# A softmax attention over eight head pairs: scores two pairs ahead, and another order of the same instructions on three engines

## The reference, cut to what matters

```python
# q: 16 heads, k and v: 2 heads (8 query heads share one), window 128, S = 256
s = jnp.einsum('bqgrd,bkgd->bgrqk', qi, ki).astype(jnp.float32) * scale
mask = (diff >= 0) & (diff < window) & (kpos[None, :] >= 0)
s = jnp.where(mask, s, NEG)
sk = sinks.astype(jnp.float32)[None, :, :, None, None]
m = jnp.maximum(jnp.max(s, axis=-1, keepdims=True), sk)
e = jnp.exp(s - m)
p = e / (jnp.sum(e, axis=-1, keepdims=True) + jnp.exp(sk - m))
o = jnp.einsum('bgrqk,bkgd->bqgrd', p.astype(vi.dtype), vi)
```

## Time and profile before

| | |
|---|---|
| median of three runs | 2857.96 us |
| the profiled execution | 2862.86 us, span 2861.1 us |
| its mean granted TensorE clock | 0.895 |
| TensorE matmuls busy | 2506.4 us (88% of the span) |
| TensorE weight loads busy | 1733.8 us (61%) |
| VectorE busy | 1243.3 us (43%) |
| ScalarE busy | 748.5 us (26%) |
| the attention that is changed, first scores to first matmul of the projection behind it | 2591.60 to 2640.20 us, 48.60 us |

### The profile page before, as it was taken

How to read it: one execution, slowest core, us unless ns; L and a number is a source line. 1 busy time by engine, 2 the same in 40 slices (tenths; PEclk the granted TensorE clock), 3 DMA queues, 4 the chain that set the end, 5 groups by cost and what they waited for, 6 DMA issues and landing times.

```text
span 2861.1 us, 34960 instructions
## 1 busy us (share of the span) xinstructions
PE 2506.4 (88%) x14300; PEld 1733.8 (61%) x14300; DVE 1243.3 (43%) x1829; ACT 748.5 (26%) x1087; POOL 21.6 (1%) x38
## 2 busy tenths in 40 slices
PE   6999777667776677799989999999989999997998
PEld 4988222112221222178677998788957888885887
DVE  2365100000000000033533776876576778775676
ACT  4332000000000000013222334434254334345333
POOL 1000000000000000000000000000000000000000
PEclk9999877777777776799899999999989999998999
DMA  8668999999999999954333554554403545551553
GB/s 314 233 244 309 416 416 418 418 418 418 416 417 418 419 419 416 416 186 162 125 118 132 191 176 165 174 199 168 148 30 119 201 166 201 181 177 60 172 181 118
DMA packets 272100, 720.69 MB, mean 252 GB/s; under 512 B 11216, under 2 KB 128992, under 8 KB 238848
## 3 DMA queue, kind: packets, MB, share of 16 engines
q1 hardware_dynamic: 270000, 708.88, 65.6%
q0 software_dynamic: 2000, 10.38, 1.0%
HBM read 716.08 MB, written 3.15 MB: 251 GB/s over the span
## 4 chain that ended last, share of the span: by engine, by line
PE 56%; DMA 18%; SPq 12%; issue 8%; DVE 3%; ACT 2%; POOL 0%; DVEq 0%; POOLq 0%; ACTq 0%
SPq L730 12%; PE bank L1329 9%; PE bank L938 7%; DMA ring<-in_w_gate_e 6%; PE bank L872 5%; PE bank L873 5%; PE bank L874 5%; DMA A<-in_w_gate_e 5%; PE bank L1330 4%; DMA xn<-in_w_up_e 4%; PE bank_pair L872 4%; PE bank_pair L873 4%; PE bank_pair L874 4%; PE bank L1143 1%; PE bank L1129 1%
## 5 line engine op out<-in xcount | busy, mean ns | idle before, releaser
L1330 PE MATMUL bank<-HT_r,ring_r 128*128 128x256 f32 x1408 | 395.9, 281 | 0.0
L1330 PEld LDWEIGHTS bank<-HT_r,ring_r 128*128 128x128 f32 x1408 | 266.8, 190 | 0.7
L2341 DVE TENSOR_TENSOR A<-bank,A 128x512 f32<-128x512 f32 x16 | 11.1, 692 | 587.6 <-PE bank L1143 587.6
L874 PE MATMUL bank<-HT_r,ring_r 128*128 128x256 f32 x904 | 255.7, 283 | 0.0
L1329 PE MATMUL bank<-HT_r,AB_r 128*128 128x512 f32 x640 | 229.7, 402 | 1.4 <-DVE HT_r L2090 1.4
L1329 PE MATMUL bank<-HT_r,AC_r 128*128 128x512 f32 x640 | 226.7, 398 | 0.0
L2082 DVE TENSOR_TENSOR ring_r<-ring,AB_r 128x2048 fp32r<-128x2048 f32 (+1 forms) x80 | 177.5, 2260 | 101.3 <-ACT AB_r L1659 101.3
L1143 PE MATMUL bank<-ring,A 128*32 128x512 f32 x768 | 141.6, 827 | 85.0 <-DMA ring<-in_w_gate_e 50.1
L2082 DVE TENSOR_TENSOR ring_r<-ring,A_r 128x2048 fp32r<-128x2048 f32 (+1 forms) x82 | 175.8, 2182 | 15.3 <-ACT A_r L1659 15.3
L874 PE MATMUL bank_pair<-A_r 128*128 128x512 f32 x456 | 178.4, 391 | 0.0
L1659 ACT ACTIVATE AB_r<-ring 128x2048 fp32r<-128x2048 f32 (+1 forms) x80 | 146.7, 1882 | 109.0 <-DMA ring<-in_w_up 36.5
(11 more groups left out here) (480 smaller groups left out, 4472.5 us busy)
## 6 DMA issues: line engine op xcount, KB each, us to landing
ring<-in_ffn_w_gu SPq DMA_DIRECT2D x88, 1024.0 KB, 6.7
ring<-in_w_up_e SPq DMA_DIRECT2D x48, 1024.0 KB, 26.6
ring<-in_w_gate_e SPq DMA_DIRECT2D x48, 1024.0 KB, 22.3
ring<-in_w_down_e SPq DMA_DIRECT2D x48, 1024.0 KB, 19.9
ring<-in_w_in SPq DMA_DIRECT2D x46, 1024.0 KB, 7.4
ring<-in_ffn_w_down SPq DMA_DIRECT2D x40, 1024.0 KB, 6.2
A<-in_w_gate_e SPq DMA_DIRECT2D x32, 1024.0 KB, 18.9
A<-in_w_up_e SPq DMA_DIRECT2D x32, 1024.0 KB, 26.7
```

The source lines that it names most:

```text
L874: return mm(out_, lhs[1], rhs[0], start=False, stop=stop, skip_group_check=True)
L1330: last = mm(both[:, 1, :], low, h_high[:, k, :], start=False, stop=(k == DC - 1), skip_group_check=True)
```

## The change

The number of instructions and every instruction stay as they are. On TensorE, scores(1) stands before the loop, and in the loop come turn(m), scores(m + 2), product(m). On ScalarE, exps(0) and exps(1) stand before the loop, and in it come copy(m), high(m), exps(m + 2). On VectorE, max(1) stands before the loop, behind the rotation, and in it come weigh(m), max(m + 2), rest(m - 1). `swa_at` and the letters of the plan follow.

```diff
--- before.py
+++ after.py
@@ -183,8 +183,10 @@
 def swa_at(m, part, i=0):
 
     if part == "scores":
-        return 4 * m - 4
-    return 4 * m + (1 if m < 7 else 0) + (i if part == "turned" else 2)
+        return 0 if m == 1 else 4 * m - 5
+    if part == "turned":
+        return 1 + 4 * min(m, 6) + 3 * max(m - 6, 0) + i
+    return swa_at(m, "turned") + (3 if m < 6 else 2)
 
 
 Q_AT, Q_ROPE_AT = (0, 1, 2, 6), (3, 4, 5)
@@ -279,7 +281,7 @@
             p.add("swa_q", "W" * 7, [1, 6], split=2)
             p.add("swa_scores0", "A")
             p.add("swa_rope3", "W")
-            p.add("swa_heads", ("A" + "WWW") * 7 + "WWW")
+            p.add("swa_heads", "A" + "WWAW" * 6 + "WWW" * 2)
             p.add("swa_out", "AA", [0, 1], split=2)
     return p
 
@@ -1585,14 +1587,15 @@
         swa_scores(0)
         copied(pe, "swa_q", Q_AT[3])
         rope("swa_rope3", 0, pairs(q3, 3))
+        swa_scores(1)
         for m in range(8):
             g = m // 4
-            if m < 7:
-                swa_scores(m + 1)
             pe.wait_ge(S["p3_ready"], 16 + m + 1)
             for d in range(2):
                 b = open_bank("swa_heads", swa_at(m, "turned", d))
                 batch(causal_blocks(b, lambda t: p3[2 * (m % 2) + t][:, d, :]))
+            if m < 6:
+                swa_scores(m + 2)
             b = open_bank("swa_heads", swa_at(m, "out"))
             for d in range(2):
                 copied(pe, "swa_heads", swa_at(m, "turned", d))
@@ -1985,14 +1988,15 @@
             run(sk[:, m % 2, :, :], sk[:, m % 2, :, :], ACT.Exp)
             exps(m % 2, (0, m % 2), 2 * (m % 2), 16 + m + 1)
 
-        swa_exps(0)
+        for m in range(2):
+            swa_exps(m)
         for m in range(8):
             for d in range(2):
                 copy_out("swa_heads", swa_at(m, "turned", d), pT3[d][:, :], n=384)
-            if m < 7:
-                swa_exps(m + 1)
             filled(act, "swa_heads", swa_at(m, "out"))
             run(o_high[:, m, :], work_bank("swa_heads", swa_at(m, "out"))[:, 0:T], ACT.Copy).then_inc(S["o_high"], 1)
+            if m < 6:
+                swa_exps(m + 2)
             if m >= 6:
                 high("swa_out", m - 6)
         ffn3(3, 11, "swa_heads", swa_at(7, "out"))
@@ -2829,14 +2833,15 @@
 
         swa_max(0)
         turned_q("swa_q", 3, "swa_rope3", 0)
+        swa_max(1)
         for m in range(8):
             rw = rw3[:, 0, m % 2, :, :]
             dve.wait_ge(S["exp3_done"], 16 + m + 1)
             link(v.tensor_tensor(rw, rs3[:, 0, m % 2, :, :], sk[:, m % 2, :, :], ALU.add))
             link(v.reciprocal(rw, rw))
             weigh((0, m % 2), 2 * (m % 2))
-            if m < 7:
-                swa_max(m + 1)
+            if m < 6:
+                swa_max(m + 2)
             if m:
                 attention_low("swa_heads", swa_at(m - 1, "out"), 8 + m, m - 1)
         low("swa_out", 0)
```

## The result

The changed kernel takes 2873.77 us (median of four runs, 2872.15 to 2877.58), against 2857.80 for the kernel before in the same session: a ratio of 1.0051, 95% interval 1.0040 to 1.0063. It is slower by half a per cent: 16.0 us between the two medians, 14.6 us by the ratio. The profiled execution has a span of 2873.1 us, 12.0 more than before.

A forecast was written before the change was run, and what follows sets the result against it. The prediction took a ring of waits across engines in the attention, none of them full, as the bound. Six rings +8.75, head +1.3 and tail 0 gave +10.0 us on the median: 2868.0 us, range 2862.5 to 2873.0.

The forecast's parts named there:

- The ring: Attention: weigh(m), turn(m), scores(m + 2), max(m + 2), rest(m - 1), weigh(m + 1) close a new one-pair ring.
- look-ahead pays: Rival, attention: the new one-pair ring does not bind; 3.66 us a pair, -7.9 us, 2850.1 us; chance 0.04.
- Its length: Attention, new ring for one pair: 5.52 us at the full clock, 7.22 at the low one, against 5.19 before.
- The mixture: Attention, six new rings: two thirds at the low clock instead of 54%, so 6.65 us a pair, +8.75 us.
- full-clock rival: Rival, attention: the clock stays full, ring 5.52 us; +2.7 us, 2860.7 us; chance 0.14.
- all-low rival: Rival, attention: the clock stays low, ring 7.22 us; +14.1 us, 2872.1 us; chance 0.12.
- Head: Start of the attention: max(1) now stands before weigh(0) on VectorE, so the first weighing comes 1.3 us later.
- tail: End of the attention: seventh turn to the slab's rounding 3.34 us against 3.53, then the same; counted as 0.
- the 0.6 for the low clock: End of the attention, seventh turn to the slab's rounding: 0.6 us more with the low clock, 0.6 less with full.
- The sum for the attention: Whole attention: six rings +8.75, first weighing +1.3, end 0, together +10.0 us.

The follow-up runs named there:

- both experiments that cut it: Against the changed kernel: scores(m + 2) ahead of turn(m) on TensorE, attention 41.65 us; weigh(m + 1) ahead of max(m + 2) on VectorE, 47.73 us.

## Why the prediction was right, and where its sizes were off

**The ring.** The step that a new ring of one pair closes over VectorE and TensorE was right, piece by piece: the two waits, the chain, and both experiments that cut it (41.65 and 47.73 us) show it, and shortening or lengthening it by one member moved it by that member (0.33 less without rest, 2.3 more with the product at the low clock). The "look-ahead pays" rival, 3.66 us a pair and 2850.1 us, is near what the order with scores ahead of turn does: 3.76 us a pair and a median of 2855.94 us, by a one-pair chain through ScalarE and not by the two-pair one of the rival. The changed kernel's scores cannot end before the weighing.

**Its length.** I put 5.52 us at the full clock and 7.22 at the low one; measured are 5.26 and, at 0.50 throughout, 6.96, both 0.26 us less. Two terms were too long. Turn and scores together were 0.88 + 1.36, but the scores start 0.71 us behind the first transpose (2616.09 to 2616.80), since their group overlaps the one ahead by more than the 0.06 I set off. And from the maximum to the next weighing it is 1.67 us (2615.93 to 2617.60), not 1.79, since VectorE's next operation starts before rest has ended by the trace; the 0.05 to the next weighing stands in none of the earlier trace rows. A third slip is that the sum has rest in all six rings, though the first has none (`if m:`): another 0.33 us too much.

**The mixture.** I took two thirds low. By the measured ends six rings would take 4.93 + 5 x 5.26 = 31.2 us all full and 6.63 + 5 x 6.96 = 41.4 all low. The 40.70 us of the first profile are then 93% low; the 38.32 and 39.06 of the other two, 70% and 77%. This error and that of the length partly cancelled, which is luck: 39.9 us were predicted for the six rings, 38.32 to 40.70 measured. The reason given, TensorE works in the low stretches and waits in the high ones, held more strongly than I let it. The full-clock rival is out: it had +2.7 us for the attention, where 8.5 to 11 were measured, and of the eighteen rings in three profiles one ran at 1.00 throughout. The Trainium skill, "TensorE: Matmul & The Clock Gate", section "Loop structure matters more than you think", which led to that rival, speaks of matmuls that follow immediately; here they wait 1.57 to 2.40 us in each ring. The all-low rival came close in the first profile for the rings.

**Head, tail, rest.** Head +1.3 was predicted and +1.29 measured, tail 0 and +0.11. That the tail came out near nothing is luck too. From the seventh pair's first transpose to the slab's rounding it is 4.08 us (2639.69 to 2643.77) against 3.53, much as the 0.6 for the low clock, named and left out, would have made it; and from the seventh weighing to that transpose it is 1.48 us against 1.90, which it did not count. What was missed besides is behind the attention: the projection starts at 0.50 for five us, another us. The sum for the attention was +10.0 against +10.95, +8.56 and +8.54 in three profiles; on the times, +10.0 against 14.6 by the ratio (four runs) and about 9 (ten runs). The time, 2873.77, lies a little above the stated range, whose upper end was 2873.0, while the ratio on the 2857.96 us that the prediction started from gives 2872.5.

## What to carry to other kernels

When groups are reordered across engines with in-order streams, follow each engine's queue past the wait: a group placed behind a waiting group inherits its wait, and if what it feeds stands ahead of that wait's source on the other engine, a ring closes that no data dependence asked for. Draw the ring for one iteration and add it up; run-ahead helps only if the group that runs ahead is issued ahead of the wait. And compare orders at equal clock before judging them: a mean granted clock says little if the engine works when it is low. When one ring is cut, look in the trace for the next: here cutting this one uncovered, in turn, a ring through ScalarE and one of copy, product, scores and turn.

## What was not expected of the hardware

- In the changed kernel's first profile the clock fell in every ring, within 0.3 us of the start of the transposes, after pauses of TensorE of 2.07 to 2.40 us (the first 3.88), although the bursts between them lasted some four us; with 1.70 us of bf16 matmuls in each pause it did not fall once in 35 us. In the run with exps ahead of high it stayed at 0.50 from 2610 to 2640, through pauses of 1.7 us.
- The same program had 57.1 to 59.6 us in the same stretch in three profiles, with rings of 5.26 and of 6.70 us beside each other in one of them; the ring of 5.26 ran at 1.00 throughout, that of 6.70 met the low clock.
- At the full clock the changed kernel's attention with 128 useless matmuls (30 and seven times 14) was 8.4 to 10.8 us shorter than without them.
